# The score matmuls of the next attention step, issued ahead of what stands beside the attention

## The chip, the cores and the metric

The kernel runs on one core of a Trainium2 chip. The metric is the device time of one launch in microseconds (us), the median of three runs. A core has TensorE (matmuls), VectorE (called DVE in the profile), ScalarE (ACT), GpSimd (POOL) and SyncE (SP, which issues the weight DMAs here). Each engine runs its own instructions strictly in the order in which the program has them, and engines wait for each other through semaphores.

## The reference

Two networks run one after the other on 256 tokens of width 1024, in float32. The first has two layers with a second stream of 256 context tokens; the second has two layers of an MLP, a mixer with three kinds of attention, a cross attention, and another MLP.

```python
def diff_attend(q, k, v, lam):                       # first network, layer 0: 8 heads, two maps each
    s = jnp.einsum('bqhmd,bkhmd->bhmqk', q, k) * ATTN_SCALE
    p = jax.nn.softmax(s, axis=-1)
    w = (p[:, :, 0] - lam * p[:, :, 1])
    return jnp.einsum('bhqk,bkhe->bqhe', w, v)       # then rms_norm of each head's output

def hybrid_mixer(h, ...):                            # second network, both layers
    o_fox = fox_attention(fq, fk, fv, log_f)         # 6 heads
    o_dsa = dsa_sparse_attention(dq, dk, dv, ...)    # 5 heads
    o_sb = stick_breaking_attention(sq, sk, sv)      # 5 heads
    g = jax.nn.sigmoid(gates)                        # 3 x 1024 columns: 24 gate tiles
    return (g0 * (o_fox @ w_fox) + g1 * (o_dsa @ w_dsa) + g2 * (o_sb @ w_sb)) @ w_out

def memory_cross_attention(h, mem_n, w_q, w_kv, w_o):  # 4 heads
    return softmax(q @ k.T * CA_HEAD_DIM ** -0.5) @ v @ w_o

mod = silu(c) @ w_mod[i] + b_mod[i]                  # 6 x 1024 columns a layer, for x and for ctx
```

## The kernel before

The program is written by hand, engine by engine. Projections run on TensorE as three matmuls with split operands (line 688), which is most of the kernel. Results go through two pools of four PSUM banks each: `A` is emptied by ACT, `V` by DVE. `take` hands out the four banks of a pool in turn; before a take TensorE waits until the bank that was taken four takes earlier has been emptied. The order of the takes is therefore part of the program.

Three places use the helper `attention`: the differential attention of the first network (32 steps, each 128 queries of one head with two maps, 512 keys in two steps of a head and 256 in the two others), the mixer (22 steps, one map, 128 or 256 keys) and the cross attention (8 steps). The work of a step is spread over several turns of the loop. Turn `i` of TensorE issues

- S(i): the scores of step i, one V bank for each map (line 653, `pv<-BIG`). The two maps of the differential attention have their 64 rows in the two halves of the array;
- T(i-2): the transposes of the probabilities, one A bank (line 658, `pa<-con,Pb`), once DVE has normalised them;
- O(i-3): probabilities times values, one V bank (line 653, `pv<-PT,BIG`), once ACT has copied T(i-3) to `PT`;
- what stands beside the attention, `also(i)`.

DVE in its turn i subtracts and takes the row maximum of S(i) (line 1823), normalises step i-1 (lines 1829 to 1836) and copies O(i-3) (line 1667). ACT in its turn i takes the exponential of step i (line 1331) and copies T(i-2) to `PT` (line 1308). All queues are in order.

Beside the differential attention stand two things. In turns 0, 1, 3, 5 and 6 of every eight, TensorE does a modulation block (`next_modulation`): a product of the condition with a raw 1 MB block of `w_mod` (line 800, `pa<-ring,BIG`), and four small matmuls that fold the block before it (`pa<-con,BIG`); two A banks. Once a head, in turn 8+4h, come the sums of a head's norm (`pa<-SQ,con`), one A bank. ACT in turn 9+4h computes the head's inverse root from it (lines 1276, 1277, 1279), DVE in turn 10+4h improves the root and scales the head (lines 1743 to 1745, 1928), ACT in turn 11+4h rounds it (line 1251, `HTh<-TMP`), DVE in turn 12+4h takes the rest (line 1692).

Beside the mixer's attention stand the index products (`index`), the stick-breaking attention (`stick`, from turn 12 on) and the gate tiles (`gate`, 24 split matmuls each, one A bank). After every second gate tile ACT and DVE split the next block of weights (lines 1245 and 1685). Beside the cross attention stand two query tiles (`last_queries`, turn 1) and a wait for their copies.

Of the kernel before, what the change touches and what calls it, by code (L numbers as in the profile page):

```python
# [28 lines left out]
P = 128  # L29
# [233 lines left out]
def program(nc, I, out):  # L263
    ctx = ExitStack()
    with ctx:
# [382 lines left out]
        def _(pe):  # L648
# [187 lines left out]
                        mm(b[:, 2 * j:2 * j + 2], modtwo[:, (n - 1) % 2, j * P:(j + 1) * P], C("fold"), True, True,  # L836
                           a_full if j else None)

            def attention(tag, kind, todo, scores, values, dv, o_rows, also=lambda i: None):

                for i in range(len(todo) + 3):
                    if i < len(todo):
                        for m in range(2 if kind == "diff" else 1):
                            pairs = scores(*todo[i], m)
                            if V.taken():
                                pe.wait_ge(v_free, V.taken())
                            b = V.take((tag, "S", i, m))
                            for j, (q, k, *where) in enumerate(pairs):
                                last = j == len(pairs) - 1
                                mm(b[:, where[0] if where else slice(0, todo[i][2])], q, k, j == 0, last,  # L850
                                   v_full if last else None)
                    if 0 <= i - 2 < len(todo):
                        u = i - 2
                        n = todo[u][2] // P
                        pe.wait_ge(pn_ready, seen.more(pn_ready))
                        if A.taken():
                            pe.wait_ge(a_free, A.taken())
                        b = A.take((tag, "T", u))
                        src = Pb[:, u % 3 * 2, :]
                        for t in range(n):  # L860
                            turn(b[:, t * P:(t + 1) * P], src[:, t * P:(t + 1) * P], a_full if t == n - 1 else None)
                    if i >= 3:
# [4 lines left out]
                        group(V, (tag, "O", u), lambda b: b[r, 0:P],  # L867
                              [(values(h, t), PT[:, u % 2, t * P:(t + 1) * P], None) for t in range(nk // P)])
                    also(i)

            def sub(h):
                return slice(h % 2 * HEAD, h % 2 * HEAD + HEAD)
# [37 lines left out]
            def first_layer(i):  # L910
# [39 lines left out]
                if i == 0:  # L950
# [3 lines left out]
                    def head_sums(step_):  # L954
# [5 lines left out]
                        if n is not None:  # L960
# [2 lines left out]
                    attention(("att", i), "diff", todo,  # L963
                              lambda h, t, n, m: [(Qa[m * HEAD:(m + 1) * HEAD, h, t * P:(t + 1) * P],
                                                   Ka[m * HEAD:(m + 1) * HEAD, h, 0:n])],
                              lambda h, t: Va[:, t, h * P:(h + 1) * P], P, lambda h: slice(0, P), head_sums)
                    for step_ in range(len(todo) + 3, HEAD_NORM_STEPS):
                        head_sums(step_)
                    N, tc = 512, ALL
# [78 lines left out]
            def mixer(l):  # L1048
# [99 lines left out]
                        group(V, ("zo", l, h), lambda b: b[r, 0:S],  # L1148
                              [(SV[:, t, h * HEAD:(h + 1) * HEAD], TMP[:, h % 2, t * S:(t + 1) * S], None) for t in range(2)])

                def beside(i):
                    if i < 2:
                        index(3 + i)
                    stick(i - STICK_FROM)
                    if gate_tile(i) is not None:
                        gate(gate_tile(i))

                attention(("mix", l, "att"), "mix", units("mix"), mix_scores, mix_values, HEAD,
                          lambda h: sub(h if h < N_FOX else h - N_FOX), beside)
                for i in range(len(units("mix")) + 3, MIX_STEPS):  # L1160
                    beside(i)
                for j in range(LATE_GATES, GATE_TILES):
                    gate(j)
                branch(0, range(2))
# [6 lines left out]
            def cross(l):  # L1171
# [10 lines left out]
                def last_queries(i):  # L1182
                    if i == 1:
                        linear(A, ("cq", l), 2, (0, P), hx, S)
                    if i == 3:
                        pe.wait_ge(a_free, A.nth((("cq", l), 3)))

                attention(("mem", l), "mem", units("mem"),
                          lambda h, t, n, m: [(CQ[:, h, t * P:(t + 1) * P], CK[:, h, 0:n])],
                          lambda h, t: CV[:, t, h * P:(h + 1) * P], P, lambda h: slice(0, P), last_queries)  # L1190
                pe.wait_ge(v_free, V.nth((("mem", l), "O", len(units("mem")) - 1)))
                for n in range(2):
                    linear(V, ("co", l), 4 * n, (0, P, 2 * P, 3 * P), quarters(lambda k: O_AT["mem"] + k), S)
# [1124 lines left out]
```

## Time and profile before

| what | us |
|---|---|
| median of three runs | 2885.19 |
| lowest and highest | 2884.97, 2889.27 |
| the profiled execution, its own time | 2884.77 |
| its span in the trace | 2882.9 |

The span counts from the first to the last recorded instruction; about 1.9 us of the launch lie outside it. The profile's page gives the busy time of each engine, 40 slices of the span, the chain of work that ended last, and the costliest groups of instructions. Answers of the trace give waits, timelines and stretches.

### The profile page before, as it was taken

What the parts mean: (1) busy time and instruction counts of PE and PEld (TensorE: products, weight loads), DVE (VectorE), ACT (ScalarE), POOL (GpSimd) and SP (SyncE); (2) the same over time, 40 slices, a digit from 0 to 9 for tenths busy, and PEclk for the clock granted to TensorE, in tenths of its full rate; (3) what the DMA queues carried; (4) which work ended last, traced back from release to release, by engine and by line L of the source; (5) the groups of instructions that cost most, each with busy time, mean ns of one, the idle gap of its engine ahead of it and who ended that gap; (6) DMA issues with size and microseconds to landing.
All of it is one profiled execution on the core that took longest, in us unless ns stands there. A gap on an engine that the chain in (4) does not pass through costs nothing.

```text
span 2882.9 us, 45579 instructions
## 1 busy us (share of the span) xinstructions
PE 2700.4 (94%) x18789; PEld 2406.9 (83%) x18789; DVE 1728.7 (60%) x3256; ACT 1284.5 (45%) x2348; POOL 128.6 (4%) x146
## 2 busy tenths in 40 slices
PE   5998889999989889999989989999999999899998
PEld 4776467888867679999989779899999997698998
DVE  4554765544566466676554766676565547666764
ACT  3544544232245454454443445554444434445543
POOL 1000000000040320000000011000000000110000
PEclk9999889999989899999999999999999999999999
DMA  7555432232252324556554314365665543144654
GB/s 243 191 175 161 146 116 74 89 102 97 93 103 88 88 76 161 166 171 183 168 158 143 111 58 147 118 172 167 189 186 165 171 138 115 58 142 126 167 167 121
DMA packets 511518, 397.09 MB, mean 138 GB/s; under 512 B 21848, under 2 KB 487008, under 8 KB 511184
## 3 DMA queue, kind: packets, MB, share of 16 engines
q1 hardware_dynamic: 508512, 387.10, 44.3%
q0 software_dynamic: 2080, 3.53, 0.9%
q8 instruction: 150, 2.46, 0.4%
q10 hardware_dynamic: 720, 3.54, 0.3%
q14 instruction: 56, 0.46, 0.0%
HBM read 393.08 MB, written 1.05 MB: 137 GB/s over the span
## 4 chain that ended last, share of the span: by engine, by line
PE 83%; DVE 9%; ACT 4%; issue 1%; POOL 1%; DMA 1%; SPq 0%; DVEq 0%; ACTq 0%
PE pv L688 42%; PE pa L688 30%; PE pv L653 5%; PE pa L653 3%; DVE Wl L1685 2%; ACT Wh L1245 1%; PE pa L800 1%; PE pa L658 1%; DMA ring<-in_w_mod_dram 1%; ACT Pb L1331 1%; DVE Lb L1823 1%; POOL BIG L2256 0%; POOL Pb L2240 0%; DVE TMP L1778 0%; DVE TMP L1756 0%
## 5 line engine op out<-in xcount | busy, mean ns | idle before, releaser
L1685 DVE TENSOR_TENSOR Wl<-ring,Wh 128x1024 fp32r<-128x1024 f32 (+3 forms) x688 | 767.6, 1157 | 350.5 <-ACT Wh L1245 348.3
L1245 ACT ACTIVATE Wh<-ring 128x1024 fp32r<-128x1024 f32 (+3 forms) x688 | 647.3, 990 | 507.7 <-PE pv L688 504.8
L688 PE MATMUL pa<-HTl,Wh 128*128 128x256 f32 (+1 forms) x1648 | 541.3, 328 | 43.9 <-DVE HTl L1763 26.7
L688 PE MATMUL pv<-HTl,Wh 128*128 128x256 f32 (+1 forms) x1872 | 547.1, 292 | 8.3 <-DVE XT L1803 2.3
L688 PE MATMUL pv<-HTh,Wl 128*128 128x256 f32 (+1 forms) x1872 | 538.3, 288 | 0.0
L688 PE MATMUL pv<-HTh,Wh 128*128 128x256 f32 (+1 forms) x1872 | 538.0, 287 | 0.0
L688 PE MATMUL pa<-HTh,Wl 128*128 128x256 f32 (+1 forms) x1648 | 525.1, 319 | 0.0
L688 PE MATMUL pa<-HTh,Wh 128*128 128x256 f32 (+1 forms) x1648 | 524.7, 318 | 0.0
L688 PEld LDWEIGHTS pa<-HTl,Wh 128*128 128x128 f32 x1648 | 325.6, 198 | 76.6 <-issue 40.9
L688 PEld LDWEIGHTS pv<-HTl,Wh 128*128 128x128 f32 x1872 | 360.4, 192 | 21.3 <-issue 7.5
L688 PEld LDWEIGHTS pv<-HTh,Wl 128*128 128x128 f32 x1872 | 360.7, 193 | 3.2 <-issue 0.5
L688 PEld LDWEIGHTS pv<-HTh,Wh 128*128 128x128 f32 x1872 | 360.6, 193 | 2.7
L688 PEld LDWEIGHTS pa<-HTh,Wl 128*128 128x128 f32 x1648 | 325.7, 198 | 20.1 <-issue 1.4
L688 PEld LDWEIGHTS pa<-HTh,Wh 128*128 128x128 f32 x1648 | 324.7, 197 | 18.5
L1308 ACT ACTIVATE BIG<-pa 128x256 f32<-128x256 f32 (+1 forms) x206 | 78.6, 387 | 311.5 <-PE pa L688 303.6
L688 PE MATMUL pv<-HID2l,Wh 128*128 128x256 f32 x704 | 199.2, 283 | 0.0
L688 PE MATMUL pv<-HID2h,Wl 128*128 128x256 f32 x704 | 199.2, 283 | 0.0
L688 PE MATMUL pv<-HID2h,Wh 128*128 128x256 f32 x704 | 199.2, 283 | 0.0
L688 PE MATMUL pv<-HID1l,Wh 128*128 128x512 f32 (+1 forms) x512 | 172.0, 336 | 0.0
L688 PE MATMUL pv<-HID1h,Wl 128*128 128x512 f32 (+1 forms) x512 | 172.0, 336 | 0.0
L688 PE MATMUL pv<-HID1h,Wh 128*128 128x512 f32 (+1 forms) x512 | 172.0, 336 | 0.0
L1793 DVE SCALAR_TENSOR_TENSOR XT<-pv,MOD,XT 128x256 f32<-128x256 f32 x216 | 95.7, 479 | 114.7 <-PE pv L688 113.9
(223 smaller groups left out, 4056.0 us busy)
## 6 DMA issues: line engine op xcount, KB each, us to landing
ring<-in_ffn_w_gu_dram SPq DMA_DIRECT2D x176, 512.0 KB, 5.1
ring<-in_w_mlp_dram SPq DMA_DIRECT2D x64, 1024.0 KB, 5.3
ring<-in_w_in_dram SPq DMA_DIRECT2D x54, 1024.0 KB, 5.2
ring<-in_w_mod_dram SPq DMA_DIRECT2D x48, 1024.0 KB, 5.7
ring<-in_ffn_w_down_dram SPq DMA_DIRECT2D x64, 704.0 KB, 4.6
ring<-in_a_w_qkv_dram SPq DMA_DIRECT2D x12, 1024.0 KB, 5.3
ring<-in_b_w_qkv_dram SPq DMA_DIRECT2D x12, 1024.0 KB, 5.2
ring<-in_w_out_dram SPq DMA_DIRECT2D x8, 1024.0 KB, 5.0
```

The lines of the kernel that those rows point to most:

```text
L653: m = nc.tensor.matmul(o, lhsT=lhsT, rhs=rhs, start=start, stop=stop)
L658: m = nc.tensor.transpose(o, x, C("ident"))
L688: m = nc.tensor.matmul(o, lhsT=x, rhs=y, start=first and j == 0, stop=last and j == 2)
L800: m = nc.tensor.matmul(b[32 * j:32 * j + 32, 0:256], lhsT=cT[:, k, :], rhs=w[:, k, :], start=k < 4, stop=k >= 4)
L1245: ins = nc.scalar.activation(Wh[rows, p % SPLIT, a:b], ring[rows, i % RING, a:b], ACT.Copy)
L1308: nc.scalar.activation(dst, src(b), func, scale=scale).then_inc(a_free, 1)
L1331: nc.scalar.activation(Pb[:, i % 3 * 2 + m, 0:n], Lb[:, i % 2 * 2 + m, 0:n], ACT.Exp, bias=nm[:, i % 2, m:m + 1], scale=-1.0, accum_out=rs ...
L1685: ins = v.tensor_tensor(Wl[rows, p % SPLIT, a:b], ring[rows, i % RING, a:b], Wh[rows, p % SPLIT, a:b].bitcast(F32), ALU.subtract)
L1793: m = v.scalar_tensor_tensor(XT[:, k, half], b[:, at:at + S], MOD[:, i, gate * KT + k, w:w + 1], XT[:, k, half], ALU.mult, ALU.add)
L1823: v.tensor_tensor_reduce(Lb[:, i % 2 * 2 + m, 0:n], b[:, 0:n], mask(*todo[i]), -scale, -NEG, ALU.add, ALU.min, nm[:, i % 2, m:m + 1]).then ...
```

## The change

`attention` gets a second callback, `behind(i)`. It is called with i-1 after the scores of step i and before T(i-2), and once more after the loop. What was passed as `also` in the differential and the cross attention is now passed as `behind`; in the mixer the stick-breaking steps stay in `also`, and index products and gate tiles go to `behind`. The wait in the cross attention moves from the end of turn 3 to the place after S(3). DVE, ACT, GpSimd and SyncE keep their order of instructions, and both pools keep their order of takes.

```diff
-            def attention(tag, kind, todo, scores, values, dv, o_rows, also=lambda i: None):
+            def attention(tag, kind, todo, scores, values, dv, o_rows, also=lambda i: None, behind=lambda i: None):
...
                                 mm(b[:, where[0] if where else slice(0, todo[i][2])], q, k, j == 0, last,
                                    v_full if last else None)
+                    if i:
+                        behind(i - 1)
                     if 0 <= i - 2 < len(todo):
...
                     also(i)
+                behind(len(todo) + 2)
...
-                              lambda h, t: Va[:, t, h * P:(h + 1) * P], P, lambda h: slice(0, P), head_sums)
+                              lambda h, t: Va[:, t, h * P:(h + 1) * P], P, lambda h: slice(0, P), behind=head_sums)
...
-                def beside(i):
+                def behind(i):
                     if i < 2:
                         index(3 + i)
-                    stick(i - STICK_FROM)
                     if gate_tile(i) is not None:
                         gate(gate_tile(i))
...
-                          lambda h: sub(h if h < N_FOX else h - N_FOX), beside)
+                          lambda h: sub(h if h < N_FOX else h - N_FOX), lambda i: stick(i - STICK_FROM), behind)
                 for i in range(len(units("mix")) + 3, MIX_STEPS):
-                    beside(i)
+                    stick(i - STICK_FROM)
+                    behind(i)
...
-                    if i == 3:
+                    if i == 2:
                         pe.wait_ge(a_free, A.nth((("cq", l), 3)))
...
-                          lambda h, t: CV[:, t, h * P:(h + 1) * P], P, lambda h: slice(0, P), last_queries)
+                          lambda h, t: CV[:, t, h * P:(h + 1) * P], P, lambda h: slice(0, P), behind=last_queries)
```

TensorE's order in the differential attention, from S(8) to S(10), in the kernel before. The rows `pv<-BIG` are scores, `pa<-con,Pb` transposes, `pv<-PT,BIG` outputs, `pa<-SQ,con` a head's sums, `pa<-ring,BIG` with `pa<-con,BIG` a modulation block:

```order
L653 MATMUL pv<-BIG 128x512 x2
L658 MATMUL pa<-con,Pb 128x128 x2
L653 MATMUL pv<-PT,BIG 128x128 x4
L653 MATMUL pa<-SQ,con 128x512
L800 MATMUL pa<-ring,BIG 32x256 x8
L653 MATMUL pa<-con,BIG 128x2 x2
L653 MATMUL pv<-BIG 128x512 x2
L658 MATMUL pa<-con,Pb 128x128 x2
L653 MATMUL pv<-PT,BIG 128x128 x2
L800 MATMUL pa<-ring,BIG 32x256 x8
L653 MATMUL pa<-con,BIG 128x2 x2
L653 MATMUL pv<-BIG 128x256 x2
```

The difference in the kernel after, at the sums of head 0 and the modulation block of turn 8:

```order
 L653 MATMUL pv<-PT,BIG 128x128 x4
+L653 MATMUL pv<-BIG 128x512 x2
 L653 MATMUL pa<-SQ,con 128x512
 L800 MATMUL pa<-ring,BIG 32x256 x8
 L653 MATMUL pa<-con,BIG 128x2 x2
-L653 MATMUL pv<-BIG 128x512 x2
```

S(9) moved ahead of the head's sums and the modulation block; T(7) and O(6) now follow directly behind that block. S(10) moves ahead of the block of turn 9 in the same way.

TensorE's order at the start of the mixer's attention, before; `pa<-BIG` are index products and `L688` the first gate tile, the `pv` rows are S(0):

```order
L653 MATMUL pa<-BIG 128x256 x4
L653 MATMUL pv<-BIG 128x128
L653 MATMUL pv<-BIG,con 128x128
L653 MATMUL pa<-BIG 128x256 x2
L688 MATMUL pa<-HTl,Wh 128x256
```

And after:

```order
L653 MATMUL pa<-BIG 128x256 x4
L653 MATMUL pv<-BIG 128x128
L653 MATMUL pv<-BIG,con 128x128
L653 MATMUL pv<-BIG 128x256
L653 MATMUL pv<-BIG,con 128x256
L653 MATMUL pa<-BIG 128x256 x2
L688 MATMUL pa<-HTl,Wh 128x256
```

S(1), two rows, moved from behind the first gate tile to in front of two index products.

## Rows read from the trace of the kernel before

**Rows 1.** The page, its chain of work that ended last, by engine

```profile
PE 83%; DVE 9%; ACT 4%; issue 1%; POOL 1%; DMA 1%; SPq 0%; DVEq 0%; ACTq 0%
```

**Rows 2.** Waits between 245 and 400 us: us in total, times, longest

```profile
DVE Lb L1823 <- PE pv L653: 57.4, 19, 25.3
ACT Pb L1331 <- DVE nm L1823: 55.8, 22, 3.9
```

**Rows 3.** Stretches: length, busy PE PEld DVE ACT POOL, clock, DMA share, GB/s

```profile
249.65:266.54 16.89, 14.06 (x128) 8.18 (x127) 9.47 (x32) 8.94 (x29) 0.00 (x0) 1.00 0.67 213
266.54:299.72 33.18, 28.09 (x209) 17.22 (x209) 24.35 (x84) 21.11 (x69) 0.00 (x0) 0.95 0.55 178
299.72:336.99 37.27, 30.69 (x210) 18.59 (x209) 26.57 (x83) 21.39 (x66) 0.00 (x0) 0.86 0.44 142
374.13:401.00 26.87, 18.42 (x108) 12.18 (x108) 20.20 (x48) 15.96 (x39) 0.00 (x0) 0.74 0.39 129
...
299.79:317.27 17.48, 15.37 (x116) 9.26 (x116) 13.54 (x42) 10.53 (x32) 0.00 (x0) 0.90 0.37 121
```

**Rows 4.** Timeline, differential attention, turns 17 to 19: start, us, engine, instruction, [idle before]

```profile
317.20 1.13 PE L653 MATMUL pv<-BIG 64*128 64x512 f32 x4
...
321.77 0.62 ACT L1279 ACTIVATE RQ<-RQ 128x512 f32<-128x512 f32 x1
322.54 1.93 PE L800 MATMUL pa<-ring,BIG 128*32 128x256 f32 x16 [3.39 <-ACT RQ L1279]
325.34 1.22 PE L653 MATMUL pv<-BIG 64*128 64x256 f32 x4
326.60 0.42 DVE L1823 CUSTOM_DVE_ANT_0 Lb<-pv,con 128x256 f32<-128x256 f32 x1 [5.03 <-PE pv L653]
```

**Rows 5.** Timeline of TensorE at full clock: modulation block, scores, transposes, output, head's sums

```profile
269.16 1.07 PE L800 MATMUL pa<-ring,BIG 128*32 128x256 f32 x16
270.70 0.70 PE L653 MATMUL pv<-BIG 64*128 64x256 f32 x4
271.33 0.66 PE L658 MATMUL pa<-con,Pb 128*128 128x128 f32 x4
271.83 0.61 PE L653 MATMUL pv<-PT,BIG 128*128 128x128 f32 x4
...
278.83 1.02 PE L653 MATMUL pa<-SQ,con 128*128 128x512 f32 x2
```

**Rows 6.** Timeline of DVE: start of a head's root, and the next scores

```profile
307.18 0.68 DVE L1743 SCALAR_TENSOR_TENSOR T<-RQ 128x512 f32<-128x512 f32 x1
...
310.02 0.42 DVE L1823 CUSTOM_DVE_ANT_0 Lb<-pv,con 128x256 f32<-128x256 f32 x1
```

**Rows 7.** Timeline of ACT: first instruction of a turn 11+4h, and of the next

```profile
310.48 0.51 ACT L1331 ACTIVATE Pb<-Lb,nm 128x256 f32<-128x256 f32 x1 [3.26 <-DVE nm L1823]
...
313.55 0.73 ACT L1331 ACTIVATE Pb<-Lb,nm 128x512 f32<-128x512 f32 x1
```

**Rows 8.** DMA issues between 245 and 400 us: KB each, median us to landing

```profile
ring<-in_w_mod_dram SPq DMA_DIRECT2D x18, 1024.0 KB, 5.1
```

**Rows 9.** A stretch of the mixer's attention in layer 0, columns as in rows 3

```profile
1615.00:1665.00 50.00, 50.00 (x339) 41.07 (x336) 38.41 (x122) 21.53 (x54) 0.00 (x0) 1.00 0.32 100
```

**Rows 10.** Timeline of TensorE: first gate tile, S(1), scores of one map, O(13)

```profile
1610.30 0.36 PE L688 MATMUL pa<-HTl,Wh 128*128 128x256 f32 x1 [1.11 <-ACT TMP L1500]
...
1613.33 0.70 PE L653 MATMUL pv<-BIG 64*128 64x256 f32 x2
...
1671.71 0.70 PE L653 MATMUL pv<-BIG 64*128 64x256 f32 x2
...
1681.73 0.65 PE L653 MATMUL pv<-PT,BIG 128*64 128x128 f32 x4 [1.09 <-ACT PT L1308]
```

**Rows 11.** Timeline of TensorE, cross attention of layer 0: S(2), T(1)

```profile
1847.25 0.60 PE L653 MATMUL pv<-BIG 128*128 128x256 f32 x2
...
1852.03 0.69 PE L658 MATMUL pa<-con,Pb 128*128 128x128 f32 x2 [3.54 <-DVE Pb L1832]
```

## The prediction

> **What bounds the kernel now.** The page's chain comes first: TensorE carries 83% of it [rows 1], so a change that only reorders TensorE can pay only where TensorE waits, or where the order makes another engine late. Then the waits, stretch by stretch. Between 245 and 400 us, the differential attention, DVE waits 57.4 us for scores; the longest single wait, 25.3 us, is DVE idling before the attention starts, so 32.1 us lie inside it. ACT waits 55.8 us behind DVE's maxima [rows 2]. There no engine is full. In eight turns (two heads) of 37.27 us DVE is busy 26.57, ACT 21.39, TensorE 30.69 at a mean granted clock of 0.86, so part of its own busy time is half clock [rows 3]. The timeline shows why. S(17) is issued at 317.20. The modulation block of turn 17 needs a bank that ACT frees only after exponential 17 and the head's root; TensorE stands 3.39 us, then does the block at half clock (1.93 us), and only then issues S(18), at 325.34. DVE, done with turn 17, waits 5.03 us for it, and ACT waits for DVE [rows 4]. The mixer is the opposite: over 50 us TensorE is busy for 50.00 us at clock 1.00 [rows 9].
>
> **The differential attention.** In the new order TensorE's turn j is S(j), block of turn j-1, T(j-2), O(j-3). S(18) then goes out before the 3.39 us wait and is there when DVE comes. I price the steady state by putting eight new turns together from single durations, measured from one start to the next.
>
> At full clock TensorE needs 1.54 us for a modulation block (269.16 to 270.70), 0.63 for scores of 256 keys, 0.50 for four transposes, 0.54 for an output of 256 keys, about 0.95 for a head's sums [rows 5], and from the widths 1.06 for scores of 512 (1.13 with its tail [rows 4]), 0.28 for two transposes, 1.0 for an output of 512. Eight turns have 5 blocks (7.7), 2 sums (1.9), scores 6.8, transposes 3.1, outputs 6.1: 25.6 us. DVE needs 26.57. So eight turns can't fall below about 26.6 us, 10.7 less than now, and the gain over the whole attention can't exceed about 43 us.
>
> The coupling that stays: a head's root costs DVE 2.84 us (307.18 to 310.02) [rows 6], in turns 2 and 6 of the eight. Behind turn 2's root comes a head with few blocks on TensorE, and DVE runs through to turn 6's root without a stop: one head's DVE work, 13.54 us [rows 3]. Behind turn 6's root the way leads through ACT. Turn 7 there is exponential, square, modulation copies, rounding (which waits for the root) and the copy of T(5): 3.07 us, from 310.48 to 313.55 [rows 7], plus 0.45 until the first maximum is there, 3.5. O(5) waits for that copy: 1.1. Then TensorE is the chain: S 1.06, sums 0.95, block 1.54, T 0.28, O 0.54, S 0.64, block 1.54, T 0.50, O 0.54, 7.6 us. DVE's copy and the next root: 0.3 + 2.84. Sum 15.4. Eight turns are 13.6 + 15.4 = 29.0 us if TensorE stays at full clock. It still stands about 2 us at T(6) and O(5), and about 1.4 us where S(4) needs the V bank that DVE is late to empty. Of what a wait does to the clock: after the 3.39 us wait the next block took 1.93 us instead of 1.07, and S(18) 1.22 instead of 0.70 [rows 4, 5]. Two shorter waits in eight turns, half of it on the chain, I put at 1.3 us (bounds 0 and 4). So 30.3 us instead of 37.27.
>
> Stretch by stretch [rows 3]. 299.72 to 374.13 is two such periods: 2 x 7.0 = 14.0 us. 266.54 to 299.72 (turns 5 to 12) has one root fewer, and 24.7 us of TensorE's own work; with about 1.5 us of waits and 0.8 for the clock it takes 27.0 instead of 33.18: 6.2 us. 249.65 to 266.54: S(1) to S(4) go ahead, TensorE's work and DVE's first latencies add to about 14.7: 2.2 us. 374.13 to 401: the last scores come a little earlier, but the end is a chain through ACT's four weight copies and the last head's root that the change doesn't touch: 1 us. Sum 23.4. The bounds: if the remaining waits cost as much as half of DVE's present 32.1 us, about 12; with every wait gone, 35.
>
> One rule of the Trainium skill speaks against this change. The two maps of a score overlap: two maps of 256 keys take 0.70 us, and so does a single map with as many rows and keys in the mixer [rows 5, 10]. Before, both maps' banks are free when S is issued, since a block lies between; now the second map's bank waits for DVE's read of the step before, and where DVE is late the first map runs alone. The Trainium skill, TensorE: Matmul & The Clock Gate, section Packing small matmuls, says that matmuls whose rows lie in distinct row groups of the array run concurrently; the trace agrees by these rows. By the rule each separated pair costs up to a score more; at one in eight turns, which is how often the turns above put DVE late (the 1.4 us include it), it changes nothing, at every turn it would be 32 x 0.8 = 26 us on TensorE, and the gain would be gone.
>
> **DMA.** Five `w_mod` blocks in 30.3 us are 6.1 us a block, against 5.1 us to landing [rows 8] with three in flight, and another stretch of this attention already moved 213 GB/s [rows 3]; the new need is 142 x 37.3/30.3 = 175. At nothing. If that cover were gone and each of the 18 blocks came 1 us late, it would be 18 us.
>
> **The mixer.** TensorE is full in its main part [rows 9], and the sum of its work stays. At the start TensorE waits for the index products' copies (1.11 us before the first gate tile) [rows 10]. S(1), 1.25 us with its second part, goes into this gap: 1.2 us a layer, 2.4 in both. Late in the attention it turns round: O(13) waits 1.09 us for ACT, whose queue holds gate tile, weight split, exponential, copy [rows 10]. That queue starts when the gate tile ends. The scores of 0.63 us now stand ahead of the gate tile, so the gate ends 0.63 later and the wait grows by as much. Where the stick-breaking product behind it waits for GpSimd anyway, this is absorbed; at one of the four gate tiles there it isn't: 0.6 a layer, 1.2 in both (bounds 0 and 5, all four).
>
> **The cross attention.** S(2), 0.43 us to the next start, now stands ahead of the two query tiles. Behind them ACT copies them and splits a block, DVE splits it, and only then takes S(2): T(1) waits 3.54 us for that [rows 11]. S(2) used to lie in this wait and now delays it: 0.43 a layer, 0.9 in both. The moved wait costs nothing: the copies are there long before S(3).
>
> Sum: -23.4 - 2.4 + 1.2 + 0.9 = -23.7 us. The profiled execution took 2884.77 us, 0.4 below the median of 2885.19, so the forecast is 2861 us.
>
> **The rivals.**
> - *The gain is real and smaller*: the in-order chains bind more than my turns show, mostly because TensorE keeps standing 1 to 2 us twice in eight turns and drops to half clock each time. With 4 us for the clock and 1.5 more of waits, eight turns take about 34.5: 2.8 x 2 + 3.5 + 1.5 = 11 us, time 2874. For it: waits of 1.2 us in this trace are also followed by slow blocks. Against: the waits that go are the long ones.
> - *Nearly DVE's bound*: TensorE no longer drops to half clock, eight turns take 27.5. 2 x 9.8 + 8 + 2.5 + 1.5 = 32 us, time 2853.
> - *Nothing*: DVE's 32.1 us of waiting come back as waits for exponentials and copies of O, which the new order puts behind the block, and the mixer loses what is left. Within 5.8 us of before, 2883. Against: DVE's turn j needs only O(j-3) from behind the block, and S(j) is there.
> - *Slower*: the clock. At half clock everywhere TensorE's 25.6 us become 51. The time of eight turns is 25.6 divided by the mean clock; it passes 37.3 when that falls below 0.69, from 0.86 now. At 0.60 it is 42.7, 5.4 more each, over four such stretches 22 us: 2907. That needs a standing TensorE in nearly every turn, for V banks with the blocks queued behind.
>
> **How the numbers follow.** Forecast 0.60, smaller gain 0.19, DVE's bound 0.12, nothing 0.06, slower 0.03. Most likely 2861 us. 2853 to 2873 leaves out the last two, and the ends of the second and third. The difference that a measurement of this kernel can tell is about 0.2%, 5.8 us. Faster 0.91, the same 0.06, slower 0.03.
>
> **What would show it.** In the new trace DVE's waits for scores in the differential attention fall from 32 us to under 12, and ACT's for the maxima with them. ACT RQ no longer stands before a wait of 3.4 us in front of line 800 with DVE idle. The distance between S(13) and S(21) falls from 37.3 to about 30. The granted clock there rises over 0.90. The waits left on TensorE are `pv<-PT` behind ACT and scores behind `nm`. The mixer's and the cross attention's stretches stay within 2 us each. Wrong would be: a distance over 34 us with the clock at 0.86 or below, or new waits of line 800 on the weights' DMA.

## The result

| | before, measured beside it | after |
|---|---|---|
| median, lowest to highest, us | 2887.23 (2884.97 to 2890.91) | 2857.82 (2852.22 to 2860.8) |
| ratio, 95% interval | | 0.9894 [0.9877, 0.9911] |
| the profiled execution, its span, us | 2884.77, 2882.9 | 2857.25, 2855.4 |
| mean granted clock | 0.964 | 0.969 |

The change saves 29 us by the medians and 27.5 us between the two profiled executions. The predicted 2861 us is 3 us above the median and inside the range of 2853 to 2873.

The chain of work that ended last, by engine, is as before [rows 1]: TensorE still bounds the whole.

```profile
PE 83%; DVE 9%; ACT 4%; issue 1%; DMA 1%; POOL 1%; SPq 0%; DVEq 0%; ACTq 0%
```

Lines are numbered up to four higher in the kernel after, and a few more in some experiments; 1827 is DVE's maximum (1823 before), 1335 the exponential (1331), 1312 the copy to `PT` (1308). The waits of the kernel after between 245 and 375 us (us in total, times, longest):

```profile
ACT Pb L1335 <- DVE nm L1827: 32.2, 19, 3.4
DVE Lb L1827 <- PE pv L653: 32.0, 12, 26.8
...
PE pv L653 <- ACT PT L1312: 8.7, 4, 4.9
DVE Oa L1671 <- PE pv L653: 8.2, 12, 2.2
...
PE pv L653 <- DVE nm L1827: 1.2, 3, 0.4
```

Against [rows 2]: without the one long wait ahead of the attention DVE now waits 5.2 us for scores instead of 32.1; ACT's wait behind the maxima fell from 55.8 to 32.2.

The stretches of the kernel after, bounded by the same instructions as in [rows 3]: to S(5), S(13), S(21), S(29), and to the last head's sums (columns as there):

```profile
250.29:264.67 14.38, 13.66 (x128) 8.11 (x127) 10.52 (x37) 10.27 (x35) 0.00 (x0) 1.00 0.71 227
264.67:291.06 26.39, 25.58 (x208) 15.71 (x207) 22.47 (x76) 18.74 (x59) 0.00 (x0) 1.00 0.62 201
291.06:320.63 29.57, 26.95 (x210) 16.24 (x209) 26.62 (x83) 21.29 (x66) 0.00 (x0) 1.00 0.55 178
320.63:351.55 30.92, 28.55 (x210) 16.95 (x209) 26.63 (x83) 21.29 (x66) 0.00 (x0) 0.94 0.53 171
351.55:376.90 25.35, 16.05 (x107) 10.70 (x106) 18.89 (x48) 16.79 (x44) 0.00 (x0) 0.84 0.46 146
```

Eight turns take 29.57 us and then 30.92, where they took 37.27, with the same 26.6 us of DVE's work in them. TensorE is busy for 26.95 us at full clock in the first, and for 28.55 at 0.94 in the second. The whole attention, from S(0) to the last head's sums, took 147.88 us and takes 125.08: 22.8 us less.

The waits that are left on TensorE stand at the two places that the prediction named. From its timeline (start, us, instruction, [idle before]):

```profile
285.78 1.12 PE L653 MATMUL pv<-BIG 64*128 64x512 f32 x2
...
287.30 1.12 PE L653 MATMUL pv<-BIG 64*128 64x512 f32 x2 [0.40 <-DVE nm L1827]
...
304.34 1.16 PE L653 MATMUL pv<-PT,BIG 128*128 128x128 f32 x8 [1.25 <-ACT PT L1312]
305.43 1.13 PE L653 MATMUL pv<-BIG 64*128 64x512 f32 x4
...
333.91 1.56 PE L653 MATMUL pv<-PT,BIG 128*128 128x128 f32 x8 [1.26 <-ACT PT L1312]
335.39 2.08 PE L653 MATMUL pv<-BIG 64*128 64x512 f32 x4
```

The first two rows are one step's two maps, separated because the second map's bank was still being read. Each takes 1.12 us by itself, as much as both together when they are issued as one (1.13) [rows 4]. This is what the row groups' rule in the Trainium skill, TensorE: Matmul & The Clock Gate, section Packing small matmuls, makes of it, and the trace agrees. It happens once in eight turns, as predicted, so it costs little. The rows at 304.34 and 333.91 us are O(5), counted within the eight turns, waiting for ACT's copy. After the first of these waits TensorE stayed at full clock (1.13 us for the scores behind it); after the second, of the same length, it fell to half clock (2.08 us for the same scores), and that is the difference between 29.57 and 30.92 us.

The mixer gained more than predicted. TensorE in layer 0 of the kernel after, at S(1) and the first gate tile, and at O(13) and O(17):

```profile
1585.52 0.70 PE L653 MATMUL pv<-BIG 64*128 64x256 f32 x2
...
1588.45 0.36 PE L688 MATMUL pa<-HTl,Wh 128*128 128x256 f32 x1 [0.98 <-ACT TMP L1504]
...
1657.34 0.65 PE L653 MATMUL pv<-PT,BIG 128*64 128x128 f32 x4 [1.87 <-ACT PT L1312]
...
1678.32 0.65 PE L653 MATMUL pv<-PT,BIG 128*64 128x128 f32 x4 [1.00 <-ACT PT L1312]
```

Answering to [rows 10]: the first gate tile still waits 0.98 us, where it waited 1.11. What S(1) fills is a wait just ahead, in front of the last two index products. In the kernel before it stood at 1608.22 us; in the kernel after these products start at 1586.77 without one:

```profile
1608.22 0.97 PE L653 MATMUL pa<-BIG 64*128 64x256 f32 x4 [0.79 <-ACT TMP L1500]
```

O(13) waits 1.87 us instead of 1.09. The last four of the 24 gate tiles follow each other behind the attention; "last gate tile" means the first of these four, the 21st, from here on. From the first to the last gate tile layer 0 took 124.93 us and takes 122.02.

The cross attention, both layers, its T(1), answering to [rows 11]:

```profile
1826.93 0.66 PE L658 MATMUL pa<-con,Pb 128*128 128x128 f32 x2 [4.02 <-issue]
...
2618.70 0.66 PE L658 MATMUL pa<-con,Pb 128*128 128x128 f32 x2 [4.02 <-issue]
```

By the lead of the kernel after over the kernel before, the 27.5 us are: 22.2 at the end of the differential attention, 24.8 at the last gate tile of layer 0, 25.6 ahead of its cross attention, 25.2 behind it, 28.1 at the last gate tile of layer 1, 28.9 ahead of its cross attention, 27.25 behind it, 27.5 at the end.

### The profile page after: what moved, and what is told of

Its sections match the earlier page's. It is cut to its first block, busy times and chain, and to the rows that moved or that the text cites. A ratio compares the mean times of both kernels' runs of the same rounds, so it can differ in the third digit from the quotient of the medians.

```text
span 2855.4 us, 45577 instructions
## 1 busy us (share of the span) xinstructions
PE 2686.0 (94%) x18789; PEld 2397.7 (84%) x18789; DVE 1726.7 (60%) x3256; ACT 1283.4 (45%) x2348; POOL 129.6 (5%) x146
## 3 DMA queue, kind: packets, MB, share of 16 engines
q10 hardware_dynamic: 720, 3.54, 0.3%
## 4 chain that ended last, share of the span: by engine, by line
PE 83%; DVE 9%; ACT 4%; issue 1%; DMA 1%; POOL 1%; SPq 0%; DVEq 0%; ACTq 0%
PE pv L688 42%; PE pa L688 31%; PE pv L653 5%; PE pa L653 3%; DVE Wl L1689 2%; ACT Wh L1249 2%; PE pa L658 1%; PE pa L800 1%; DMA ring<-in_w_mod_dram 1%; DVE Lb L1827 1%; POOL Pb L2244 0%; DVE TMP L1782 0%; DVE T L1748 0%; DVE TMP L1760 0%; DVE HTl L1767 0%
## 5 line engine op out<-in xcount | busy, mean ns | idle before, releaser
L688 PE MATMUL pa<-HTl,Wh 128*128 128x256 f32 (+1 forms) x1648 | 539.5, 327 | 43.9 <-DVE HTl L1767 26.9
L688 PE MATMUL pv<-HTl,Wh 128*128 128x256 f32 (+1 forms) x1872 | 545.9, 292 | 9.1 <-DVE XT L1807 2.2
L688 PE MATMUL pv<-HTh,Wl 128*128 128x256 f32 (+1 forms) x1872 | 537.0, 287 | 0.0
L688 PE MATMUL pv<-HTh,Wh 128*128 128x256 f32 (+1 forms) x1872 | 536.6, 287 | 0.0
L688 PE MATMUL pa<-HTh,Wl 128*128 128x256 f32 (+1 forms) x1648 | 524.1, 318 | 0.0
L688 PE MATMUL pa<-HTh,Wh 128*128 128x256 f32 (+1 forms) x1648 | 523.7, 318 | 0.0
L688 PEld LDWEIGHTS pa<-HTl,Wh 128*128 128x128 f32 x1648 | 324.2, 197 | 79.8 <-issue 43.3
L688 PEld LDWEIGHTS pv<-HTl,Wh 128*128 128x128 f32 x1872 | 358.9, 192 | 22.5 <-issue 7.4
L688 PEld LDWEIGHTS pv<-HTh,Wl 128*128 128x128 f32 x1872 | 359.2, 192 | 3.2 <-issue 0.5
L688 PEld LDWEIGHTS pv<-HTh,Wh 128*128 128x128 f32 x1872 | 359.1, 192 | 2.7
L688 PEld LDWEIGHTS pa<-HTh,Wl 128*128 128x128 f32 x1648 | 324.5, 197 | 19.7 <-issue 1.4
L688 PEld LDWEIGHTS pa<-HTh,Wh 128*128 128x128 f32 x1648 | 323.7, 196 | 18.5
L688 PE MATMUL pv<-HID2l,Wh 128*128 128x256 f32 x704 | 199.2, 283 | 0.0
L688 PE MATMUL pv<-HID2h,Wl 128*128 128x256 f32 x704 | 199.2, 283 | 0.0
L688 PE MATMUL pv<-HID2h,Wh 128*128 128x256 f32 x704 | 199.2, 283 | 0.0
L688 PE MATMUL pv<-HID1l,Wh 128*128 128x512 f32 (+1 forms) x512 | 172.0, 336 | 0.0
L688 PE MATMUL pv<-HID1h,Wl 128*128 128x512 f32 (+1 forms) x512 | 172.0, 336 | 0.0
L688 PE MATMUL pv<-HID1h,Wh 128*128 128x512 f32 (+1 forms) x512 | 172.0, 336 | 0.0
```

The source lines that it names most:

```text
L688: m = nc.tensor.matmul(o, lhsT=x, rhs=y, start=first and j == 0, stop=last and j == 2)
```

## The experiments

Each kernel was timed beside the kernel before; the ratio is that of the two, with its 95% interval.

| kernel | new order in | median, us | before | ratio |
|---|---|---|---|---|
| e8_after | all three places | 2857.2 | 2886.18 | 0.9901 [0.9888, 0.9914] |
| e1_diff | differential attention | 2863.26 | 2888.15 | 0.9909 [0.9885, 0.9933] |
| e6_root_turns | the same, blocks of turns 1 mod 4 alone | 2881.54 | 2888.15 | 0.997 [0.9957, 0.9982] |
| e2_mix | mixer | 2877.97 | 2888.15 | 0.9965 [0.995, 0.9981] |
| e10_mix_start | mixer, turns 0 and 1 | 2888.33 | 2889.82 | 1.0005 [0.9995, 1.0016] |
| e11_mix_main | mixer, turns 0 to 11 | 2883.11 | 2889.82 | 0.9988 [0.9975, 1.0001] |
| e4_t_first | none; T ahead of S in the mixer | 2891.08 | 2888.15 | 1.0007 [0.9993, 1.0022] |
| e3_cross | cross attention | 2889.75 | 2886.18 | 1.0014 [1.0004, 1.0023] |
| e9_cross_old | all but the cross attention | 2852.54 | 2889.82 | 0.9875 [0.9859, 0.9892] |
| e5_round_late | all, and ACT's rounding moved | 2856.02 | 2886.18 | 0.9894 [0.988, 0.9908] |
| e7_all | all but cross, rounding moved | 2847.52 | 2886.18 | 0.9866 [0.9853, 0.9879] |

The kernel after once more, as what the later ones are compared with:

> The kernel after once more, on the chip of the three others, as what they are compared with. Both theories: 26 to 30 us below before, ratio 0.989 to 0.991; the cross attention's wait in front of T(1) 4.0 us in both layers.

Its medians repeat: 29.0 us below before.

**The differential attention alone.** In the kernel after, the mixer and the cross attention are put back.

```diff
-                          lambda h: sub(h if h < N_FOX else h - N_FOX), lambda i: stick(i - STICK_FROM), behind)
+                          lambda h: sub(h if h < N_FOX else h - N_FOX), beside)
...
-                              lambda h, t: CV[:, t, h * P:(h + 1) * P], P, lambda h: slice(0, P), behind=last_queries)
+                              lambda h, t: CV[:, t, h * P:(h + 1) * P], P, lambda h: slice(0, P), last_queries)
```

> The new order in the differential attention alone; mixer and cross attention as in the kernel before. Theory (the gain is DVE's earlier start on the scores there): the distance S(13) to S(21) is 29.6 us as after and not 37.3, the time is 22 to 24 us below before, and the mixer's stretches are those of before, gate tile to gate tile 4.88 us on the mean. Rival (a good part of the measured 29 us comes from elsewhere in this stretch's shadow, through the clock or the weights' DMA further on): 27 us or more below before.

S(13) to S(21) and S(21) to S(29) in its trace:

```profile
292.10:321.67 29.57, 26.94 (x209) 16.24 (x208) 26.62 (x83) 21.30 (x66) 0.00 (x0) 1.00 0.56 179
321.67:352.72 31.05, 28.55 (x210) 16.99 (x209) 26.65 (x83) 21.31 (x66) 0.00 (x0) 0.95 0.52 169
```

The same two stretches as with the whole change, 29.57 us at full clock and one of 31.05 with half clock in it; the attention takes 125.45 us. By the medians it saves 25 us of the 29, in runs that lie up to 8 us apart. So most of the gain is made here.

**Only the scores behind a head's sums.** Is it the one long wait, or the order of every block? Here the scores go ahead only of what stands in turns 1 mod 4, at whose end the waits of 3.4 us stood.

```diff
-                              lambda h, t: Va[:, t, h * P:(h + 1) * P], P, lambda h: slice(0, P), behind=head_sums)
+                              lambda h, t: Va[:, t, h * P:(h + 1) * P], P, lambda h: slice(0, P),
+                              lambda i: None if i % 4 == 1 else head_sums(i), lambda i: head_sums(i) if i % 4 == 1 else None)
```

> Differential attention alone, and there the scores go ahead only of the block of turns 1, 5, 9, ..., the one that may wait for the bank that the head's root frees; ahead of all other blocks and of the head's sums they stay behind, as before. Theory A (the loss was the scores' standing behind the wait for the root and the half clock after it): eight turns take 32 to 33 us, 14 to 17 us below before in all, two thirds of what the full order gives. Theory B (every block ahead of scores costs its own length, wherever it stands): 2 of 5 blocks and none of the 2 sums are passed, a third of the work, so eight turns take 34.8 us and the gain is 7 us.

Its S(13) to S(21), and two rows of its timeline:

```profile
301.10:337.30 36.20, 30.85 (x210) 19.08 (x209) 25.90 (x82) 21.03 (x63) 0.00 (x0) 0.86 0.43 140
```

```profile
284.19 0.69 DVE L1828 CUSTOM_DVE_ANT_0 Lb<-pv,con 128x512 f32<-128x512 f32 x1 [2.60 <-PE pv L653]
...
288.25 1.93 PE L800 MATMUL pa<-ring,BIG 128*32 128x256 f32 x16 [2.62 <-ACT RQ L1284]
```

Eight turns take 36.2 and 35.0 us, and the whole 6.6 us less than before. The gain is the 7 us of theory B, and theory A's 14 to 17 us are ruled out. B's reason, the length of what is passed, isn't shown by that; the rows show another. The wait in front of line 800 only shrinks from 3.3 to 2.6 us, because the root that it hangs on stands in ACT's queue behind the exponential of S(9), and S(9) itself still came behind the sums and the block of turn 8. A step that stands late anywhere in the eight turns makes the root late again. The order pays when it holds in every turn.

**The mixer alone.** The kernel after with the two other places put back.

```diff
-                              lambda h, t: Va[:, t, h * P:(h + 1) * P], P, lambda h: slice(0, P), behind=head_sums)
+                              lambda h, t: Va[:, t, h * P:(h + 1) * P], P, lambda h: slice(0, P), head_sums)
```

(and the cross attention as in the experiment above)

> The new order in the mixer alone. By the prediction's terms: 0.6 us a layer gained, 1.2 in all. By the trace after: 2.95 us a layer, 6 us in all, of which 1.25 at the start and 0.13 a step between full gate tiles.

From the first gate tile of layer 0 to 0.07 us behind the start of the last:

```profile
1615.13:1737.29 122.16, 114.40 (x714) 92.53 (x714) 86.81 (x238) 53.88 (x130) 14.95 (x10) 0.96 0.27 83
```

From start to start it is 122.09 us, 2.8 less than the 124.93 of before, and the time falls by 10 us (span 2875.6, 7.3 less), far more than twice 2.9. That the surplus is the order's own isn't shown: in this trace layer 0's mixer begins 4.8 us later than before, though nothing ahead of it was changed, and layer 1's takes 120.05 us instead of 124.99, at a clock of 0.97 instead of 0.93 behind turn 11. The rest was won between the two. How much half clock a trace has is taken up by the last experiments.

**Why a full TensorE got faster.** In the main part TensorE never stands [rows 9], with the same instructions before and after, and yet gate tiles follow each other after 4.745 us instead of 4.885. A pair of stretches shows where, first before, then after: the gate tile's last row, what follows it, and the output.

```profile
1627.06 0.28 PE L688 MATMUL pa<-HTh,Wh 128*128 128x256 f32 x1
1627.27 0.48 PE L653 MATMUL pv<-BIG 64*128 64x128 f32 x2
...
1628.10 0.33 PE L658 MATMUL pa<-con,Pb 128*128 128x128 f32 x1
1628.35 0.65 PE L653 MATMUL pv<-PT,BIG 128*64 128x128 f32 x4
```

```profile
1604.69 0.28 PE L688 MATMUL pa<-HTh,Wh 128*128 128x256 f32 x1
1604.82 0.27 PE L658 MATMUL pa<-con,Pb 128*128 128x128 f32 x1
1605.02 0.65 PE L653 MATMUL pv<-PT,BIG 128*64 128x128 f32 x4
```

Scores start 0.21 us after a gate tile's last matmul starts, transposes 0.13 us; and from transposes to outputs it is 0.25 and 0.20. That is 0.13 us a turn for a change of neighbours. To test it without the change, the kernel before gets T(i-2) ahead of S(i) in the mixer:

```diff
+                    def issue_scores():
...
+                    def issue_transposes():
...
+                    for issue in (issue_transposes, issue_scores) if kind == "mix" else (issue_scores, issue_transposes):
+                        issue()
```

> The kernel before, with one swap in the mixer's attention: T(i-2) is issued ahead of S(i) and not behind it. No scores come earlier; each comes about 0.3 us later. Theory (on a full TensorE the gain of a step is one of neighbours: transposes right behind a gate tile cost 0.13 us less than scores behind the gate tile and transposes behind the scores): gate tile to gate tile 4.75 us on the mean as after, 1.3 us a layer gained up to turn 11. Rival (the gain of a step comes from scores that are issued earlier): 4.88 us as before, or more.

Between the fifth and the eleventh, gate tiles follow each other after 4.74 us on the mean, against 4.885 before and 4.745 after, though no scores come earlier: the neighbours are the cause. The time doesn't move, since the part behind turn 11 lost 2.6 us again, 74.52 us instead of 71.95. TensorE's waits, 8.1 us instead of 7.5, account for 0.6 us of it (three new ones of 0.56 us for DVE's probabilities among them). Most of it is half clock: the granted clock there is 0.89 instead of 0.93.

**Parts of the mixer.** With the kernel before, first only turns 0 and 1 in the new order, then turns 0 to 11.

```diff
-                          lambda h: sub(h if h < N_FOX else h - N_FOX), beside)
+                          lambda h: sub(h if h < N_FOX else h - N_FOX), lambda i: (stick(i - STICK_FROM), behind(i) if i >= 2 else None),
+                              lambda i: behind(i) if i < 2 else None)
```

(12 in place of 2 in the second)

> Before, with the new order only for what stands beside turns 0 and 1 of the mixer: S(1) ahead of two index products and the first gate tile, S(2) ahead of the second. By the prediction's term (S(1) fills the wait for the index products' copies): the stretch from the first to the last gate tile as before, 125.0 us, since the gain lies ahead of the first gate tile's start or is seen as S(1) missing behind it; from the mixer's start to the tenth gate tile 1.2 to 1.4 us less than before in each layer, gate tiles 4.88 us apart as before, the time 2.4 to 3 us below before. Rival (the gain at the start is given back at the first wait behind, O(13) waiting longer): under 1 us.

> Before, with the new order for turns 0 to 11 of the mixer and the old one from turn 12 on, where the stick-breaking steps run. Theory (the gain is the start, 1.25 us, and the shorter step on a full TensorE, 0.135 us for each of ten turns; the late turns give nothing): gate tiles 4.75 us apart up to turn 11, the last one 2.6 us earlier than before as with the whole mixer in the new order, O(13) waiting 1.1 us as before. Rival A (the late turns' new order is needed, since the product behind them no longer waits for GpSimd only because its scores come earlier): 1 us or more of the 2.9 is lost by the last gate tile. Rival B (the late turns cost 0.6 us as the prediction's sum has it): the last gate tile comes 0.5 us or more earlier than with the whole mixer in the new order.

| layer 0, us from the attention's index projections | before | turns 0, 1 | turns 0 to 11 | all turns |
|---|---|---|---|---|
| first gate tile | 21.39 | 21.38 | 21.37 | 21.37 |
| tenth | 64.60 | 63.19 | 63.21 | 63.24 |
| gate tile of turn 11 | 74.37 | 72.96 | 72.29 | 72.32 |
| last | 146.32 | 147.16 | 146.44 | 143.46 |

The start is worth 1.41 us and the neighbours 0.67 more up to turn 11. But with the late turns in the old order these gains are gone at the last gate tile, which comes 0.8 us later than before with two turns and 0.1 with twelve. TensorE's waits there don't explain it: together they are 7.5 us before, 6.7 with two turns, 7.5 with twelve. The clock does: behind turn 11 it is 0.93 before and with all turns, 0.89 with two and 0.88 with twelve. The stretches around the first and second step of the stick-breaking, first in the kernel before, then with turns 0 to 11:

```profile
1682.00:1692.50 10.50, 9.67 (x49) 7.39 (x48) 7.13 (x17) 3.70 (x11) 2.17 (x1) 0.84 0.32 101
1694.50:1700.50 6.00, 5.24 (x34) 4.56 (x34) 2.98 (x6) 1.54 (x6) 1.98 (x2) 1.00 0.00 0
```

```profile
1679.50:1690.00 10.50, 9.67 (x42) 7.96 (x42) 6.13 (x12) 2.93 (x8) 2.16 (x1) 0.67 0.32 101
1694.00:1700.00 6.00, 5.79 (x30) 5.38 (x30) 2.28 (x5) 0.21 (x2) 1.43 (x2) 0.72 0.00 0
```

Around two waits of about the same length, for ACT's copy (1.09 us in both) and for GpSimd (0.81 and 0.76), TensorE ran at half clock for 7.0 us instead of 3.6 (read in stretches of 0.2 us), and for another 3.6 us a little later, where before had none. Both expectations were wrong there: the first kernel's gain holds up to the tenth gate tile and is then given back, as its rival had it, but to the clock and not to O(13), which still waits 1.09 us; of the second kernel rival A is right that more than 1 us is lost without the late turns, but not in its reason, the wait for GpSimd. The time of the second kernel falls by 0.12%, with an interval that just reaches no change; that of the first doesn't fall.

**The cross attention alone, and everything but it.** First the kernel before with the new order there, then the kernel after with the old one.

```diff
-                    if i == 3:
+                    if i == 2:
...
-                              lambda h, t: CV[:, t, h * P:(h + 1) * P], P, lambda h: slice(0, P), last_queries)
+                              lambda h, t: CV[:, t, h * P:(h + 1) * P], P, lambda h: slice(0, P), behind=last_queries)
```

> The new order in the cross attention alone (differential attention and mixer as before). Theory (the scores of step 2 used to lie inside the wait of T(1) and now stand ahead of the query tiles that this wait hangs on): the wait in front of T(1) grows from 3.54 to about 4.0 us in both layers, from the cross attention's scores to its output projection each layer gets 0.4 to 0.5 us longer, the whole 0.9 us slower than before, with up to 1.2 us a layer either way by the place where the half clock behind the wait ends. Time between 0 and 3 us above before. Rival (nothing: the second query tile's copy and the weight split are not what T(1) waits for): the wait stays 3.54 us. Second rival (the cross attention in the kernel after lost its time to the clock alone, not to the order): wait 4.0 us, but the stretch as long as before.

> The kernel after with nothing but the cross attention in its old order. It splits the 8.5 us by which the run with the rounding moved and the old cross attention was faster than the one with the rounding alone. Theory (the cross attention's old order is what pays: its wait in front of T(1) is 0.48 us shorter, and with the mixer in the new order the half clock behind this wait lasts 3.6 us instead of 7.0 in layer 0, with shorter stretches of half clock at the two later stops of the layer too): from the mixer's start in layer 0 to the cross attention's output in layer 1 it takes 1057.2 us as in that run, against 1063.7 in the kernel after; the time 5 to 8 us below after. Rival (what pays is the pair of both changes, since the place of the half clock hangs on all that stands before): less than 3 us below after.

In the first, T(1) waits 4.01 us in both layers instead of 3.54. The span grows by 1.7 us, the median by 3.6 with an interval of 1 to 7. From T(1) to the first matmul of the output product, layers 0 and 1, first in the kernel before, then with the new order there, then in the kernel after but for the cross attention:

```profile
1852.03:1864.22 12.19, 11.27 (x55) 9.02 (x55) 8.97 (x38) 6.71 (x21) 0.00 (x0) 0.75 0.32 87
2647.16:2658.10 10.94, 10.02 (x55) 7.71 (x55) 8.69 (x38) 6.71 (x21) 0.00 (x0) 0.87 0.36 97
```

```profile
1852.86:1864.86 12.00, 11.09 (x54) 8.83 (x54) 8.83 (x38) 6.67 (x20) 0.00 (x0) 0.76 0.32 87
2648.10:2660.13 12.03, 11.11 (x54) 8.86 (x54) 8.83 (x38) 6.67 (x20) 0.00 (x0) 0.76 0.33 89
```

```profile
1829.02:1840.09 11.07, 10.15 (x54) 7.82 (x54) 8.70 (x38) 6.72 (x21) 0.00 (x0) 0.85 0.35 96
2614.89:2626.98 12.09, 11.17 (x55) 8.91 (x55) 8.88 (x38) 6.72 (x21) 0.00 (x0) 0.76 0.32 88
```

Besides the 0.48 us of the wait, each layer takes either 11.0 us at a clock of about 0.86 or 12.1 at 0.75, by how long half clock lasts behind the wait. Of 18 layers with the old order, in the traces of nine kernels, ten are of the shorter kind; of eight layers with the new order, in four traces, none. The kernel without it takes 1057.4 us from the mixer of layer 0 to this output product of layer 1, against 1063.7 in the kernel after; the expectation said 1057.2. The time is 5 us below that of the kernel after, which ran on other chips, the ratio 0.9875 against 0.9901 and 0.9894, with intervals that still overlap; the last experiment is the clearer one. Of the 6.4 us between the traces only 1.0 is the two waits. Another 1.0 is the shorter half clock right behind the first of them. 2.5 lie between the cross attention of layer 0 and the mixer of layer 1, where at two stops half clock lasts 3.6 and 7.0 us instead of 7.0 and 10.4, and 2.0 in that mixer, whose instructions are the same in both.

**The rounding behind the copy.** In the new order ACT's rounding of a head, which waits for its root, stands ahead of the copy that O(5) waits for.

```diff
-                        h = head_norm(step_, 11)
-                        if h is not None:
-                            rounded(HTh[:, h, :], TMP[:, h % 2, :])
 
-                    attention(("att", i), "diff", todo, head_norms)
+                    def head_rounded(step_):
+                        h = head_norm(step_, 11)
+                        if h is not None:
+                            rounded(HTh[:, h, :], TMP[:, h % 2, :])
+
+                    attention(("att", i), "diff", todo, head_norms, head_rounded)
...
                         head_norms(step_)
+                        head_rounded(step_)
```

> The kernel after, with one thing moved: in the differential attention ACT rounds a head (HTh<-TMP, which waits for the head's root from DVE) behind its copy of T instead of in front of it. Theory (in the new order the chain of eight turns runs from the second root through ACT's rounding and its copy of T to the output product; the rounding is in it only because it stands in front of the copy): the waits of 1.2 us in front of pv<-PT at 304.3, 333.9 and 364.8 go, eight turns take about 28 us instead of 29.6 and 30.9, the attention 3 to 6 us less, the time 3 to 6 us below after. Rival A (DVE's own work is the bound now: eight turns hold 26.6 us of it, and TensorE's 25.6 us leave no room): under 1.5 us gained. Rival B (the rounding only moves: the rest of the head, which DVE takes from the rounded one, comes later, and DVE then stands at it with the maxima behind it): eight turns 30 to 32 us, the time the same as after or up to 3 us above it, and waits of DVE behind HTh appear.

Its S(13) to S(21) to S(29), and O(5) behind S(16):

```profile
290.62:319.68 29.06, 26.95 (x209) 16.24 (x208) 26.55 (x83) 21.30 (x66) 0.00 (x0) 1.00 0.56 180
319.68:348.74 29.06, 26.95 (x210) 16.25 (x209) 26.55 (x83) 21.30 (x66) 0.00 (x0) 1.00 0.56 183
```

```profile
303.38 1.16 PE L653 MATMUL pv<-PT,BIG 128*128 128x128 f32 x8 [0.74 <-ACT PT L1312]
```

The wait shrinks from 1.25 to 0.74 us, half clock is gone from both stretches, and the attention takes 120.80 us, 4.3 less. The theory is right on the chain and too large on the period, 29.06 instead of 28. In the timed runs only 1.2 us are left of it against the kernel after on the same chip, with intervals that overlap, so they show no gain; that is the size that rival A named, and they can't tell the two apart. Part of the difference is the clock again, elsewhere. Two stretches of the kernel after, first in the profiled execution of the result, then in that of the repetition:

```profile
1113.00:1123.00 10.00, 8.71 (x71) 8.33 (x72) 4.95 (x13) 2.30 (x5) 0.00 (x0) 1.00 0.33 105
1141.00:1151.00 10.00, 9.71 (x68) 9.32 (x69) 3.41 (x7) 4.46 (x14) 0.00 (x0) 1.00 0.35 109
```

```profile
1113.00:1123.00 10.00, 8.54 (x57) 8.15 (x58) 4.58 (x11) 0.81 (x2) 0.00 (x0) 0.83 0.33 105
1141.00:1151.00 10.00, 8.04 (x40) 7.10 (x41) 3.64 (x5) 5.11 (x13) 0.00 (x0) 0.83 0.50 168
```

The same kernel runs there at 1.00 once and at 0.83 the other time. The profiled execution with the rounding moved has half clock at both places as well. Such stretches come and go between executions and blur a gain of 4 us.

**Both.**

> The rounding moved as in the run before, and the cross attention in its old order; mixer and differential attention in the new order. Theory (the new order costs 0.5 us a layer in the cross attention and pays in the two other places): 1 to 2 us below the kernel that has only the rounding moved, 4 to 8 us below after. Rival (the cross attention's order is worth nothing, the differences of its stretch come from the clock): the same as that kernel within 0.5 us.

2847.52 us, all four runs within 1.5 us: 9.7 us below the kernel after on the same chip, 38.7 below before. It is the fastest version found, and it was expected to gain less than it did. Against the kernel with the rounding moved alone it is 8.5 us less, on the same chip and with intervals that don't overlap: this is the clearest evidence that the cross attention is better left in its old order.

## Why the prediction was right

- *The differential attention, -23.4.* Measured -22.8. The distance S(13) to S(21) was put at 30.3 us: it is 29.57 and 30.92, mean 30.25. That it fits so well is in part luck. At full clock the turns were added up to 29.0 us and took 29.57, 0.6 more; the clock was put at 1.3 us a period and cost nothing in the first and 1.35 in the second, 0.7 on the mean. The two misses cancel. Turns 5 to 12 took 26.39 instead of 27.0, the start 2.5 less instead of 2.2 (14.38 against 16.89). The end was put at 1 us less and took 0.4 more: 25.35 us, where it took 24.94.
- *What would show it.* DVE's waits fell to 5.2 us (under 12 expected), the clock in the first full stretch is 1.00 (over 0.90), O(5) and the second map of S(4) wait, no block waits for its weights. One sign failed: the mixer's stretches were to stay within 2 us and moved by 2.9.
- *DMA, at nothing.* 178 GB/s against the 175 worked out, and no wait.
- *The mixer, -2.4 + 1.2.* The start has the right size, 1.2 us expected a layer and 1.41 measured, though the wait that S(1) fills is the 0.79 us in front of the index products and not the 1.11 us in front of the first gate tile, which is still 0.98. The sentence "the sum of its work stays" is the mis-sized step. The work of a full TensorE shrank by 0.13 us a turn, since what a matmul costs depends on its neighbour. And the late turns, put at 0.6 us lost, gained 0.8 (71.14 us behind turn 11 instead of 71.95, at the same clock of 0.93): O(13) and O(17) wait 0.78 and 0.77 us longer, but za0, the first stick-breaking product, no longer waits for GpSimd (0.81 before), and the third's wait fell from 2.30 to 1.81 (all waits there 7.5 us before, 7.7 after), so that TensorE's own work shrank there as well. 2.9 us a layer were gained instead of 0.6.
- *The cross attention, +0.9.* The wait grew by 0.48 us a layer, 0.43 expected. Not in the sum was what follows it: the longer half clock, up to 1.2 us a layer, and more further on. With it this part of the change costs some 5 us in the kernel after, and 8.5 beside the moved rounding.
- *The sum, -23.7, against -27.5 in the trace.* The mixers gave 4.6 us more than their term. Another 1.6 came where half clock appeared twice between the mixer and the cross attention of each layer before, and once now. The cross attentions cost 2.1 instead of 0.9, the differential attention gave 0.6 less, and 0.7 went elsewhere: -23.7 - 4.6 - 1.6 + 1.2 + 0.6 + 0.7 = -27.4. That the whole is so near to the forecast is again misses of either sign; the half clock outside the differential attention was in no term.
- *The rivals.* "Nothing" and "slower" needed waits to come back; they didn't. The range's lower end at DVE's bound wasn't reached: eight turns hold 26.6 us of DVE's work and take 29.57 us at best, 29.06 with the rounding moved.

## What to carry to other kernels

In an in-order queue the instruction that another engine is waiting for goes ahead of the filler work, at every step, since one late step makes the next shared resource late again; count the filler's own waits too, not only its work. Where the next step's input used to lie inside somebody's wait, moving it ahead makes that wait longer, so such an order has to be tried place by place: here it paid where engines wait in turn, and cost time where one long wait is a chain by itself. A term of one microsecond can be worth several or nothing at all once half clock is behind it, so small steps have to be judged on the whole kernel, in more than one execution.

## What the runs showed of the hardware

- The price of a matmul depends on what stands in front of it, on an engine that never stands: 0.21 us from a gate tile to scores, 0.13 to transposes; 0.25 us from transposes to outputs behind scores, 0.20 behind a gate tile. In the mixer's full part this is about 0.13 us of every 4.88.
- A wait of 1.25 us is followed by full clock in one period and by half clock in the next (the rows at 304.34 and 333.91 us). Half clock behind the same wait of the same instruction lasted 3.6 or 7.0 us, and at one later stop 7.0 or 10.4, in two kernels whose orders differ only in a cross attention some 500 us earlier. The executions of one kernel differ by it as well: before ran between 2881 and 2895 us in these comparisons. What decides it wasn't settled.
